# Prompt attention of a hybrid decoder: a step takes two query heads of each key head instead of four of one

## The reference, cut to what matters

```python
qb = q.reshape(B, nb, qb_size, N_KV_HEADS, GROUP, HEAD_DIM)            # 2 key heads x 4 query heads
s = jnp.einsum('bnqkgd,bnskd->bnkgqs', qb, kb) * (HEAD_DIM ** -0.5)
s = jnp.where(valid, s, NEG_INF)
m = jnp.maximum(jnp.max(s, axis=-1), sink)
p = jnp.exp(s - m[..., None])
denom = jnp.sum(p, axis=-1) + jnp.exp(sink - m)
p = p / denom[..., None]
o = jnp.einsum('bnkgqs,bnskd->bnqkgd', p, vb)
...
branches = jnp.stack([o_a, o_b, o_c, o_d], axis=2)                      # o is o_c
merged = jnp.einsum('blrd,blrd->bld', sigmoid(gates), einsum(branches, w_branch))
x = x + merged @ w_out
```

## Time and profile before

| | |
|---|---|
| median of three runs | 2087.77 us |
| the profiled execution | 2088.41 us |
| its span, first to last instruction | 2086.4 us |
| TensorE (PE) busy | 2036.1 us, 98% |
| VectorE (DVE) busy | 1225.7 us, 59% |
| ScalarE (ACT) busy | 787.3 us, 38% |
| GpSimd (POOL) busy | 380.6 us, 18% |
| mean busy share of the DMA engines | 31% |

### The profile page before, as it was taken

One profiled execution on the slowest core, in us unless ns is written; L12 is line 12 of the kernel. 1 busy time (PEld: TensorE's weight loads), 2 busy tenths in 40 slices (PEclk: granted clock), 3 DMA queues, 4 the chain that ended last, 5 costly groups with the idle time before them and its releaser, 6 DMA issues.

```text
span 2086.4 us, 38895 instructions
## 1 busy us (share of the span) xinstructions
PE 2036.1 (98%) x16516; PEld 1982.0 (95%) x16516; DVE 1225.7 (59%) x1667; ACT 787.3 (38%) x1209; POOL 380.6 (18%) x238
## 2 busy tenths in 40 slices
PE   6989999999999999999989999999999999999998
PEld 6989889999999999999989998899999999999998
DVE  4897667765556453345539975677555565533445
ACT  4323442643543432233233144435535333322332
POOL 0695000211104000000307930003111030000003
PEclk9999999999999999999999999999999999999999
DMA  7523323123222222222444243222223232222223
GB/s 237 97 84 82 71 72 109 67 92 102 105 99 85 98 95 89 99 81 78 139 120 88 91 62 82 73 100 82 94 82 122 82 101 101 75 93 95 101 76 127
DMA packets 70038, 199.54 MB, mean 96 GB/s; under 512 B 41554, under 2 KB 42706, under 8 KB 51408
## 3 DMA queue, kind: packets, MB, share of 16 engines
q1 hardware_dynamic: 26144, 177.50, 25.6%
q10 hardware_dynamic: 43760, 20.11, 5.4%
HBM read 187.42 MB, written 12.29 MB: 96 GB/s over the span
## 4 chain that ended last, share of the span: by engine, by line
PE 43%; DVE 5%; issue 1%; ACT 1%; POOL 0%; DVEq 0%; POOLq 0%
PE acc L604 40%; DVE cacc L1263 1%; DVE wlo L1269 1%; PE m L698 1%; PE m L687 1%; DVE q L1260 1%; ACT tmp L947 0%; DVE sct L1263 0%; PE m L711 0%; PE m L618 0%; DVE gt L1260 0%; PE m L813 0%; PE m L785 0%; PE m L823 0%; PE m L663 0%
## 5 line engine op out<-in xcount | busy, mean ns | idle before, releaser
L604 PE MATMUL acc<-xhi,wlo 128*128 128x260 f32 x3680 | 754.5, 286 | 28.7 <-PEq L567 19.5
L604 PE MATMUL acc<-xhi,whi 128*128 128x260 f32 x3680 | 743.8, 284 | 0.0
L604 PE MATMUL acc<-xlo,whi 128*128 128x260 f32 x3680 | 742.7, 283 | 0.0
L604 PEld LDWEIGHTS acc<-xhi,wlo 128*128 128x128 f32 x3680 | 571.7, 190 | 46.3 <-issue 40.0
L604 PEld LDWEIGHTS acc<-xhi,whi 128*128 128x128 f32 x3680 | 569.6, 189 | 0.0
L604 PEld LDWEIGHTS acc<-xlo,whi 128*128 128x128 f32 x3680 | 569.3, 189 | 0.0
L1269 DVE TENSOR_TENSOR wlo<-raw,whi 128x1024 fp32r<-128x1024 f32 (+3 forms) x344 | 434.4, 1271 | 36.2 <-ACT whi L964 34.8
L964 ACT ACTIVATE whi<-raw 128x1024 fp32r<-128x1024 f32 (+3 forms) x344 | 332.1, 994 | 255.2 <-PE acc L604 197.9
L947 ACT ACTIVATE gt<-gt 128x520 f32<-128x520 f32 x226 | 144.4, 639 | 215.0 <-DVE gt L1260 210.2
L1260 DVE TENSOR_TENSOR gt<-acc,rstd 128x520 f32<-128x520 f32 x80 | 55.9, 699 | 216.0 <-PE acc L604 195.7
L604 PE MATMUL acc<-hhi,whi 128*128 128x260 f32 x704 | 141.5, 282 | 0.0
(11 more groups left out here) (224 smaller groups left out, 2132.6 us busy)
## 6 DMA issues: line engine op xcount, KB each, us to landing
raw<-in_wt SPq DMA_DIRECT2D x142, 1024.0 KB, 4.8
raw<-in_wt SPq DMA_DIRECT2D x16, 768.0 KB, 4.3
raw<-in_wt SPq DMA_DIRECT2D x16, 640.0 KB, 3.9
x<-yt ACTq DMA_DIRECT2D x2, 2080.0 KB, 9.4
yt<-x ACTq DMA_DIRECT2D x16, 260.0 KB, 2.1
x<-in_xt SPq DMA_DIRECT2D x4, 520.0 KB, 5.0
yt<-in_xt SPq DMA_DIRECT2D x1, 2080.0 KB, 16.1
s<-in_gs ACTq DMA_DIRECT2D x4, 512.0 KB, 3.6
```

Source lines behind the costliest of these rows:

```text
L604: ins = nc.tensor.matmul(out[:, h], a, b[:, h * TH:h * TH + TH], start=first and n == 0, stop=last and n == 2)
```

## The change

A step now takes two query heads of each of the two key heads: block g // 2, head pair g % 2. Its four score matmuls go h by h through both key heads, so that they alternate between the row halves of the array; key head 0 writes bank 0, key head 1 bank 1. For each key block the value work is two matmuls of 256 columns, one per key head, on the two column halves, instead of one of 512. The copy of the result is 128 partitions by 256 instead of 64 by 512, and VectorE reads the sinks as a 2 by 2 view. The slots, waits and signals stay.

```diff
                         for g in range(NBLK * NKV):
-                            blk, kv = g // NKV, g % NKV
-                            rows = slice(kv * HEAD, kv * HEAD + HEAD)
+                            blk = g // 2
                             k0 = 0 if blk else 1
                             if n == ATT[g] + 3:
                                 pe.wait_ge(s["a_tc"], g + 1)
                                 for kc in range(k0, 2):
-                                    ins = nc.tensor.matmul(m4[rows, 2], vb[:, blk - 1 + kc, rows], probt[:, kc],
-                                                           start=kc == k0, stop=kc == 1)
+                                    for kv in range(NKV):
+                                        rows = slice(kv * HEAD, kv * HEAD + HEAD)
+                                        ins = nc.tensor.matmul(m4[rows, 2, 0:2 * P], vb[:, blk - 1 + kc, rows],
+                                                               probt[:, kc, kv * 2 * P:kv * 2 * P + 2 * P],
+                                                               start=kc == k0, stop=kc == 1)
                                 ins.then_inc(s["a_o"], 1)
...
                             if n == ATT[g]:
                                 if g:
                                     pe.wait_ge(s["a_max"], g)
-                                for h in range(GROUP):
-                                    ins = nc.tensor.matmul(
-                                        m4[:, h // 2, (h % 2) * 256 + k0 * P:(h % 2) * 256 + 256],
-                                        q[rows, h, blk * P:blk * P + P],
-                                        kt[rows, (blk - 1 + k0) * P:(blk + 1) * P], start=True, stop=True)
+                                for h in range(2):
+                                    for kv in range(NKV):
+                                        rows = slice(kv * HEAD, kv * HEAD + HEAD)
+                                        ins = nc.tensor.matmul(
+                                            m4[:, kv, h * 256 + k0 * P:h * 256 + 256],
+                                            q[rows, g % 2 * 2 + h, blk * P:blk * P + P],
+                                            kt[rows, (blk - 1 + k0) * P:(blk + 1) * P], start=True, stop=True)
                                 ins.then_inc(s["a_s"], 1)
...
                             if n == ATT[g] + 4:
                                 a.wait_ge(s["a_o"], g + 1)
-                                act(q[rows, :, blk * P:blk * P + P],
-                                    m4[rows, 2].rearrange("p (h n) -> p h n", h=GROUP), name="a_out")
+                                act(q[:, g % 2 * 2:g % 2 * 2 + 2, blk * P:blk * P + P],
+                                    m4[:, 2, 0:2 * P].rearrange("p (h n) -> p h n", h=2), name="a_out")
...
-                                st.need(tt(rmax, rmax, par_("sink", kv * GROUP, GROUP), ALU.max))
-                                tt(esink, par_("sink", kv * GROUP, GROUP), rmax, ALU.subtract)
+                                rmax2 = rmax.rearrange("p (v h) -> p v h", v=NKV)
+                                st.need(tt(rmax2, rmax2, sinks, ALU.max))
+                                tt(esink.rearrange("p (v h) -> p v h", v=NKV), sinks, rmax2, ALU.subtract)
```

More of the change, by code:

```diff
@@ L1365, in side @@
                         for g in range(NBLK * NKV):
-                            blk, kv = g // NKV, g % NKV
+                            blk = g // 2
+                            sinks = par_("sink", 0, NKV * GROUP).rearrange("p (v h) -> p v h", v=NKV)\
+                                [:, :, g % 2 * 2:g % 2 * 2 + 2]
                             w = slice(0 if blk else P, 2 * P)
```

## The result

Four runs of the changed kernel gave a median of 2065.69 us (2064.17 to 2065.76), four of the kernel before, in turn with them, 2087.77 us (2087.36 to 2089.17). The ratio is 0.9892, with a 95% interval of 0.988 to 0.9905: 22.1 us, or 1.1%, faster. The forecast was 2065.7 us. Another set of runs on another chip gave 2065.55 (2064.55 to 2066.33) against 2088.03, ratio 0.989 (0.9875 to 0.9906). The profiled execution took 2065.61 us with a span of 2063.8.

The account below looks back on a forecast made before the run. TensorE, busy 98% of the span, was taken to set the time. Scores 11.9 us plus values 11.9 less 1.7 of waiting at step 1 gave 22.1 off 2087.77: 2065.7 us, range 2062.5 to 2073.5.

Parts of the forecast that it names:

- The steps: Score and value steps on TensorE: both array halves work in parallel, only streaming halves; scores gain 11.9 us, values 11.9.
- The scaling from the 128-column step of the GLA mixer to 256 columns: Score steps of 256 columns: 1.92 to 1.07 us, by scaling the GLA step's measured saving; gain 10.2 us.
- that from small tiles to 128 rows with column halves: Value steps: column halves overlap as line 750's 64-row, 64-column tiles seem to; 0.425 us per key block, 11.9 in all.
- The rivals of the array: TensorE's score and value steps: columns not overlapping (chance 0.06), weight loads exposed (0.06), turns between halves stopping the array (0.03).
- Columns that don't overlap: Value steps: column halves do not overlap with 128 rows, values gain nothing; 11.0 us gained, 2076.7 us; chance 0.06.
- turns that stop the array: Score and value steps: halves do not overlap, each of 88 turns costs 0.24 us; 21 us slower, 2109 us; chance 0.03.
- Exposed weight loads: Value steps: a 0.136 us load shows before each of 56 pairs, losing 7.6 us; 2073.3 us; chance 0.06.
- The loss at step 1: TensorE's wait for VectorE's probabilities at attention step 1 grows by 0.86 us per layer, 1.7 us in all.
- a rival, for step 2: VectorE's backlog reaches attention step 2, for instance through GpSimd's work beside it; at most 2.6 us, 2068.3 us; chance 0.05.
- Step 2: Attention step 2: VectorE's probabilities still end at least 1.1 us before TensorE comes, so no loss is counted.
- the sum: Whole program: 11.9 us from scores plus 11.9 from values less 1.7 at step 1, 22.1 us faster, 2065.7 us.

Follow-up runs that it names:

- the kernel with the pause: Changed kernel with GpSimd's convolution stopped before tap 16 until VectorE takes the 28th chunk from `acc`, and attention step 6 one slot earlier: 2048.9 us.

## Why the prediction was right

**The steps.** Their prices, read as a fixed part and 0.105 us per 128 columns, and the halves taken as wholly parallel, came out within 0.01 us for all four shapes. With waits taken off, attention is 12.0 us shorter per layer. The scaling from the 128-column step of the GLA mixer to 256 columns, and that from small tiles to 128 rows with column halves, were inferences; both held. The change itself is thus explained by the array: the halves of its rows, or of its columns, work beside each other when one step has work for both.

**The rivals of the array.** Columns that don't overlap would have left the value step at 1.86 us, turns that stop the array would have lengthened both; at 1.01 us neither is so. Exposed weight loads would have shown as 0.136 us per pair; the value step of two key blocks is no longer than half the old stream plus its fixed part, 0.85 + 0.16 us. For them stood the rule of the Trainium skill, page "TensorE: Matmul & The Clock Gate", section Part 3: Packing small matmuls, that a weight load overlaps only where the row group differs, and its factor for three column tiles, from which the prediction estimated a gain of 8.8 us for the values. For two column halves of 64 with all 128 rows the measurement decides against both: the gain is 28 x 0.425, 11.9 us.

**The loss at step 1: right place, wrong size.** The step reads "VectorE's stretch can only start earlier by what TensorE has gained before it, 0.43 us", so 0.86 us of loss per layer. Measured it is 1.65 - 0.43 = 1.22 and, in layer 2, 1.62 - 0.32 = 1.30: 2.5 us instead of 1.7. The start of the stretch did gain what was forecast: it lies 7.20 us behind the first scores before (170.32 - 163.12) and 6.76 after (168.70 - 161.94), 0.44 less. What failed is the length, which I had taken for fixed. From that start to the end of step 1's probabilities VectorE needs 20.44 us before and 20.80 after, in layer 2 20.33 and 20.77. The 0.36 and 0.44 us are just what the loss exceeds the forecast by. In layer 1 they lie in the two taps, 2.67 us instead of 2.31, which take 1.41 us when GpSimd has stopped: VectorE's operations beside GpSimd's change in length with how the two fall against each other. GpSimd, which I had named only in a rival, for step 2, is thus what keeps VectorE late: without its work there the wait is gone, the 0.43 us of before included.

**Step 2.** The room was to be at least 1.1 us. The probabilities end at 202.28 in the profile after, TensorE comes at 203.56: 1.28 us. No further wait came, as forecast.

**Why the sum still came out.** By the attention parts alone the profiled change is 10.8 and 12.2 us, and of the latter 1.6 belong to a stretch of low clock in the profile of before: 21.4 us, not 22.1. The 0.7 missing are the step 1 term. The rest up to the 22.6 us between the spans is made of things that the change doesn't touch: stretches of low clock that one profile has and the other hasn't, and a wait at line 669, 1.8 us before and 0.4 after (the changed kernel with the values grouped has 1.8 us there too). The agreement of the medians to 0.1 us is thus better than the working deserves; the working was good to about 1 us.

## What to carry to other kernels

Where small matmuls use one half of the array's rows or columns, put independent work for the other half next to it, in any order; read the step's price from first start to the next group's start, split it into a fixed part and a part per column, and halve only the latter. Then look at who is late: when TensorE gains 1 us between two points, the engine that feeds it must gain as much between the same points or have that much room. And where small VectorE operations show several times their usual length, look at GpSimd in the same microseconds before moving anything else: work of GpSimd that nobody waits for can still lengthen the program, here by 12 us or more, and putting it later took one wait.

## What the runs showed of the hardware that I had not expected

- **GpSimd stretches VectorE far beyond its own share.** 8-column operations go from 0.22 to 1.26 us. With half of GpSimd's convolution put later, the program is 12.2 us shorter than the kernel that has step 6 early only (2061.13 to 2048.9, on two chips).
- **A stretch of half clock may follow a wait of TensorE, and in the same place may not.** The mean granted clock of TensorE is in the third column from the right of these rows, which give busy times of each engine in a stretch behind step 1's wait, here 1.65 and 1.66 us long. The profile after, and that of the changed kernel run again:

```profile
190.80:194.30 3.50, 3.50 (x32) 3.17 (x29) 2.76 (x5) 1.13 (x2) 0.00 (x0) 1.00 0.02 5
```

```profile
190.80:194.30 3.50, 3.50 (x17) 2.70 (x15) 2.76 (x6) 1.13 (x2) 0.00 (x0) 0.52 0.00 0
```

The second is the lower level, 1.2 of 2.4 GHz: 17 matmuls instead of 32, and the score step of 256 columns takes 1.79 us instead of 1.07 (190.50 to 192.29). Such a stretch costs about 1.6 us: in those two profiles the attention part of layer 1 is 141.99 and 143.60 us. The same stands behind the 3.6 us wait at line 663, whose matmuls take 3.44 us in the profile after and 1.96 in that of before, in layer 1. In the kernel with the pause, where both waits are gone or short, neither place has it. A stretch more or less may explain a spread of 2 us between runs, and part of what the removed waits brought seems to be that no such stretch followed there. But it comes without a wait too. In the profile after the clock falls near 494 us, 0.9 us behind matmuls of 8 rows, with no idle time of TensorE over 0.1 us in the 10 us before:

```profile
491.08 1.94 PE L816 MATMUL m<-vbd,tmp 8*64 8x512 f32 x8
```

```profile
493.90:497.20 3.30, 3.30 (x18) 3.30 (x17) 2.47 (x7) 0.00 (x0) 0.00 (x0) 0.50 0.57 238
```

The same group of matmuls ends near 495 us in the changed kernel run again, and there the clock stays up. Why a stretch comes in one place and not in another stays open.
